# A decoder kernel on one core: dilation stage with its value step one tile later and stores on GpSimd; layer 1's output stage weighs a cached sequence at another place, with six slots

## The reference

```python
qb = to_res(q)                       # rows regrouped by residue mod d, blocks of 128
kk, vv = with_prev(to_res(k)), with_prev(to_res(v))   # own and previous block
s = jnp.einsum('brnqhe,brnkhe->brnhqk', qb, kk)
s = jnp.where(valid, s, NEG)         # rel >= 0 and rel <= window // d
m = jnp.max(s, axis=-1, keepdims=True)
p = jnp.exp(s - m)
l = jnp.sum(p, axis=-1, keepdims=True)
o = jnp.einsum('brnhqk,brnkhe->brnqhe', p / l, vv)
```

## Time and profile before

| what | value |
|---|---|
| median of 3 runs | 3226.03 us (3225.46 to 3228.44) |
| profiled execution, its own time | 3226.22 us |
| span in its trace, first to last instruction | 3224.6 us |
| mean granted TensorE clock | 0.974 of full speed |
| busy: TensorE, its weight loads, VectorE, ScalarE, GpSimd | 3021.1, 2481.6, 1254.7, 1036.8, 342.7 us |
| dilation stage, first load issued to first turn of the next stage | 2590.7 to 2886.4 us |
| layer 1's output stage, to the end | 2886.4 to 3224.6 us |

### The profile page before, as it was taken

One profiled execution on the slowest core, in us unless ns is written; L12 is line 12 of the kernel. 1 busy time (PEld: TensorE's weight loads), 2 busy tenths in 40 slices (PEclk: granted clock), 3 DMA queues, 4 the chain that ended last, 5 costly groups with the idle time before them and its releaser, 6 DMA issues. The chain is left out here.

```text
span 3224.6 us, 39799 instructions
## 1 busy us (share of the span) xinstructions
PE 3021.1 (94%) x14734; PEld 2481.6 (77%) x14734; DVE 1254.7 (39%) x2917; ACT 1036.8 (32%) x3236; POOL 342.7 (11%) x457
## 2 busy tenths in 40 slices
PE   7999999998997999979999999999889978869999
PEld 6788888886886888867888888888678767757777
DVE  4322222222335543344122222333332457756665
ACT  5211111111333242244021211333222357755642
POOL 0000000000110000000011011111332134430000
PEclk9999999999998999989999999999999989988999
DMA  4110111111234433142222221221663345554552
GB/s 141 37 40 30 40 32 37 37 32 37 88 131 155 143 133 102 66 146 88 69 76 69 72 73 68 75 74 67 155 170 124 125 143 176 185 179 158 188 172 94
DMA packets 159684, 324.88 MB, mean 101 GB/s; under 512 B 19184, under 2 KB 36144, under 8 KB 159528
## 3 DMA queue, kind: packets, MB, share of 16 engines
q1 hardware_dynamic: 136936, 253.25, 24.7%
q0 software_dynamic: 22592, 69.56, 6.2%
HBM read 223.58 MB, written 99.16 MB: 100 GB/s over the span
## 5 line engine op out<-in xcount | busy, mean ns | idle before, releaser
L109 PE MATMUL ps<-prepb_wh,b_xthi 128*128 128x512 f32 x784 | 309.6, 395 | 23.9 <-DVE tokb_o L878 15.3
L109 PE MATMUL ps<-b_wh,b_xthi 128*128 128x512 f32 x784 | 308.0, 393 | 6.7 <-DVE tokb_o L878 5.3
L110 PE MATMUL ps<-prepb_wl,b_xthi 128*128 128x512 f32 x784 | 307.5, 392 | 0.0
L111 PE MATMUL ps<-prepb_wh,b_xtlo 128*128 128x512 f32 x784 | 307.4, 392 | 0.0
L111 PE MATMUL ps<-b_wh,b_xtlo 128*128 128x512 f32 x784 | 306.4, 391 | 0.0
L110 PE MATMUL ps<-b_wl,b_xthi 128*128 128x512 f32 x784 | 306.3, 391 | 0.0
L786 ACT ACTIVATE tokb_o<-ps 128x128 f32<-128x128 f32 (+1 forms) x484 | 126.7, 276 | 437.2 <-PE ps L111 359.6
L109 PE MATMUL ps<-a_xthi,prepa_wh 128*128 128x512 f32 x512 | 200.6, 392 | 5.8 <-DVE prepa_wl L103 5.8
L109 PE MATMUL ps<-a_xthi,a_wh 128*128 128x512 f32 x512 | 201.1, 393 | 4.0 <-DVE a_xtlo L222 4.0
L110 PE MATMUL ps<-a_xtlo,prepa_wh 128*128 128x512 f32 x512 | 200.4, 391 | 0.0
L111 PE MATMUL ps<-a_xthi,prepa_wl 128*128 128x512 f32 x512 | 200.2, 391 | 0.0
(11 more groups left out here) (353 smaller groups left out, 6426.9 us busy)
## 6 DMA issues: line engine op xcount, KB each, us to landing
kv_dram<-tokb_o POOLq DMA_DIRECT2D x96, 256.0 KB, 2.3
tok_b_dram<-tokb_o POOLq DMA_DIRECT2D x96, 256.0 KB, 2.6
tokb_raw<-w_b_dram SPq DMA_DIRECT2D x88, 256.0 KB, 3.0
conv_raw<-w_a_dram SPq DMA_DIRECT2D x64, 256.0 KB, 3.4
grp_dram<-dil_o SPq DMA_DIRECT2D x48, 260.0 KB, 2.1
out_grp<-grp_dram SPq DMA_DIRECT2D x48, 260.0 KB, 4.3
dil_q<-tok_b_dram SPq DMA_DIRECT2D x48, 256.0 KB, 3.0
dil_k<-kv_dram SPq DMA_DIRECT2D x48, 256.0 KB, 3.5
```

Of the source, the lines that this page charges most:

```text
L109: pe.matmul(acc, a_hi, b_hi, start=first, stop=False)
L110: pe.matmul(acc, a_hi, b_lo, start=False, stop=False)
L111: return pe.matmul(acc, a_lo, b_hi, start=False, stop=last)
```

## The change

In the dilation stage:

- The value step comes one turn later: in the turn of s TensorE makes the scores of s-1, turns s, makes the sums of s-3 and turns the probabilities of s-2. ScalarE first makes the halves of q and k of s, then all exponentials of s-1, the copy of the sums of s-3, and the probabilities of s-2. VectorE makes the low probabilities of s-3, adds the sums of s-4, then all minima of s-1.
- SyncE only loads: q and k of s, then v of s-1. The stores are issued by GpSimd: in its body for tile s, after the value split of s, it waits for o_done of s-2 and stores tile s-2.
- VectorE's minima of a tile wait for the store of the tile four before, then for the scores, and begin with a memset of one column of a new small tile, once per half.

In layer 1's output stage:

- The ring has six slots (two new ones of 3 x 512 columns beside the four in the spare operands); the pair of t+1 is loaded in SyncE's iteration t.
- ScalarE weighs the first of pair t+1 between the exponentials and the high half of the turned probabilities of step t. Layer 0's output stage keeps its order.

The diff, without the list of semaphore names (which gains v_in4 and v_in5):

```diff
@@ -1023,7 +1023,6 @@
-    RING = 4
@@ -1035,6 +1034,7 @@
+        self.RING = 4 if self.conv else 6
 
@@ -1050,7 +1050,9 @@
         else:
+            ring = core.sb(st, f"{tag}_ring", [P, 2, 3, C])
             self.ring = [x[:, 3 * n:3 * n + 3, C:2 * C] for x in (spare0, spare1) for n in range(2)]
+            self.ring += [ring[:, n, :, :] for n in range(2)]
@@ -1422,7 +1424,7 @@
                 if conv and t < 4:
                     for j in (2 * t, 2 * t + 1):
                         keys.load(sp, j)
-                for v in pair_at(t):
+                for v in pair_at(t if conv else t + 1):
                     dec.load(sp, v)
                 if t == 0:
                     dec.small_loads(sp)
@@ -1492,12 +1494,14 @@
                     e = act.activation(prob[:, h, :], ps[:, 1 + h // 2, (h % 2) * MEM:(h % 2 + 1) * MEM], ACT.Exp,
                                        scale=SCALE, bias=stat[:, 1, h:h + 1], accum_out=stat[:, 2, h:h + 1])
                 e.then_inc(exped, 1)
+                for v in pair_at(t + 1)[:1] if not conv else ():
+                    dec.weigh(act, v)
                 act.wait_ge(pturned, t + 1)
                 act.activation(pt_hi, p_turned, ACT.Copy).then_inc(phi_done, 1)
                 if not conv:
                     act.wait_ge(mturned, t + 1)
                     act.activation(cat_hi[:, u, 0:H, :], turned_heads, ACT.Copy).then_inc(mhi_done, 1)
-                for v in pair_at(t + 1)[:1]:
+                for v in pair_at(t + 1)[:1] if conv else ():
                     dec.weigh(act, v)
             for t in range(NT):
                 step(t)
@@ -1861,6 +1865,7 @@
+        scratch = core.sb(st, "dil_scratch", [P, 2 * U])
@@ -1890,9 +1895,11 @@
 
         @block.sync
         def _(sp):
-            def store(s):
-                sp.wait_ge(o_done, cnt(s))
-                sp.dma_start(rows(dst[s[0]], *s), o_b[:, s[2], :]).then_inc(o_out[s[2]], 16)
+            def load_v(s):
+                g, _, u = s
+                if back(s, U):
+                    sp.wait_ge(vlo_done, cnt(back(s, U)))
+                sp.dma_start(v_b[:, u, :], rows(kv_src[g][:, C:2 * C], *s)).then_inc(v_in[u], 16)
 
             def body(*s):
                 g, _, u = s
@@ -1900,16 +1907,10 @@
                     sp.wait_ge(turned, cnt(back(s, U)))
                 sp.dma_start(q_b[:, u, :], rows(q_src[g], *s)).then_inc(qk_in[u], 16)
                 sp.dma_start(k_b[:, u, :], rows(kv_src[g][:, 0:C], *s)).then_inc(qk_in[u], 16)
-                if back(s, U):
-                    sp.wait_ge(vlo_done, cnt(back(s, U)))
-                sp.dma_start(v_b[:, u, :], rows(kv_src[g][:, C:2 * C], *s)).then_inc(v_in[u], 16)
-                if back(s, 3):
-                    store(back(s, 3))
+                if back(s, 1):
+                    load_v(back(s, 1))
             turns(sp, body)
-            for k in (3, 2, 1):
-                store(back(END, k))
-            for s in o_out:
-                sp.wait_ge(s, 16 * TURNS * GROUPS)
+            load_v(back(END, 1))
 
         @block.gpsimd
         def _(pool):
@@ -1920,6 +1921,10 @@
                 cols = masks[:, at * P:(at + 1) * P]
                 pool.affine_select(out=cols, in_=cols, compare_op=ALU.is_ge, fill=NEG, base=0,
                                    pattern=[[-sign, P]], channel_multiplier=sign).then_inc(masked, 1)
+
+            def store(s):
+                pool.wait_ge(o_done, cnt(s))
+                pool.dma_start(rows(dst[s[0]], *s), o_b[:, s[2], :]).then_inc(o_out[s[2]], 16)
 
             def body(*s):
                 u = s[2]
@@ -1932,7 +1937,13 @@
                 pool.wait_ge(vhi_done, cnt(s))
                 pool.tensor_tensor(v_hl[:, slot, :, 1, :], v, v_hl[:, slot, :, 0, :], ALU.subtract
                                    ).then_inc(vlo_done, 1)
+                if back(s, 2):
+                    store(back(s, 2))
             turns(pool, body)
+            for k in (2, 1):
+                store(back(END, k))
+            for s in o_out:
+                pool.wait_ge(s, 16 * TURNS * GROUPS)
 
         @block.scalar
         def _(act):
@@ -1956,41 +1967,45 @@
                 act.wait_ge(pturned, half_cnt(s, half))
                 act.activation(pt_hi[:, heads, a:b, :], turned_p[:, heads, a:b, :], ACT.Copy).then_inc(phi_done, 1)
 
+            def probs(s):
+                for half in range(2):
+                    probs_high(s, half)
+
             def body(*s):
-                one = back(s, 1)
-                if one:
-                    exps(one, 0)
+                one, two, three = (back(s, k) for k in (1, 2, 3))
                 act.wait_ge(turned, cnt(s))
                 act.activation(qt_hi[:, :], ps[:, 0, :], ACT.Copy).then_inc(qhi_done, 1)
                 act.activation(kt_hi[:, :, s[2] % 2, :], ps[:, 5, :].rearrange("p (h k) -> p h k", h=H), ACT.Copy
                                ).then_inc(khi_done, 1)
                 if one:
+                    exps(one, 0)
                     exps(one, 1)
-                    probs_high(one, 0)
-                    probs_high(one, 1)
-                if back(s, 2):
-                    copy_sums(back(s, 2))
+                if three:
+                    copy_sums(three)
+                if two:
+                    probs(two)
             turns(act, body)
-            last = back(END, 1)
-            for half in range(2):
-                exps(last, half)
-            for half in range(2):
-                probs_high(last, half)
-            copy_sums(back(END, 2))
-            copy_sums(last)
+            one, two, three = (back(END, k) for k in (1, 2, 3))
+            exps(one, 0)
+            exps(one, 1)
+            copy_sums(three)
+            probs(two)
+            copy_sums(two)
+            probs(one)
+            copy_sums(one)
 
         @block.vector
         def _(dve):
-            def wait_scores(s, half):
-                dve.wait_ge(scored, half_cnt(s, half))
-                if half == 0 and back(s, U):
-                    dve.wait_ge(o_out[s[2]], use(back(s, U)))
-
             def minima(s, half):
+
                 a, b = span(s)
                 u, slot = s[2], s[2] % 2
+                if half == 0 and back(s, U):
+                    dve.wait_ge(o_out[u], use(back(s, U)))
+                dve.wait_ge(scored, half_cnt(s, half))
+                dve.memset(scratch[:, 2 * u + half:2 * u + half + 1], 0.0)
                 for h in (2 * half, 2 * half + 1):
                     m = dve.tensor_tensor_reduce(
                         prob[:, slot, h, a:b, :].rearrange("p s k -> p (s k)"),
@@ -2013,16 +2028,13 @@
                 dve.tensor_tensor(o, sums_hl[:, :, 1, :], o, ALU.add).then_inc(o_done, 1)
 
             def attend(s):
-                one, two, three = (back(s, k) for k in (1, 2, 3))
-                for half in range(2):
-                    if one:
-                        wait_scores(one, half)
-                    if two:
-                        probs_low(two, half)
-                    if one:
-                        minima(one, half)
-                    if three and half == 0:
-                        add_sums(three)
+                one, three, four = (back(s, k) for k in (1, 3, 4))
+                for half in range(2 if three else 0):
+                    probs_low(three, half)
+                if four:
+                    add_sums(four)
+                for half in range(2 if one else 0):
+                    minima(one, half)
 
             def body(*s):
                 attend(s)
@@ -2034,11 +2046,11 @@
             dve.wait_ge(masked, 3)
             turns(dve, body)
             attend(END)
-            last = back(END, 1)
-            for half in range(2):
-                probs_low(last, half)
-            add_sums(back(END, 2))
-            add_sums(last)
+            for k in (2, 1):
+                for half in range(2):
+                    probs_low(back(END, k), half)
+                add_sums(back(END, k + 1))
+            add_sums(back(END, 1))
 
         @block.tensor
         def _(pe):
@@ -2091,19 +2103,22 @@
                         t.then_inc(pturned, 1)
 
             def body(*s):
-                if back(s, 1):
-                    score(back(s, 1))
+                one, two, three = (back(s, k) for k in (1, 2, 3))
+                if one:
+                    score(one)
                 turn(s)
-                if back(s, 2):
-                    sums(back(s, 2))
-                if back(s, 1):
-                    turn_probs(back(s, 1))
+                if three:
+                    sums(three)
+                if two:
+                    turn_probs(two)
             turns(pe, body)
-            last, before = back(END, 1), back(END, 2)
-            score(last)
-            sums(before)
-            turn_probs(last)
-            sums(last)
+            one, two, three = (back(END, k) for k in (1, 2, 3))
+            score(one)
+            sums(three)
+            turn_probs(two)
```

(9 more changed lines are left out.)

## The result

The changed kernel takes **3295.65 us** (median of four runs, 3291.33 to 3302.84) against 3226.97 (3225.46 to 3228.44): a ratio of 1.0215, 95% interval 1.0195 to 1.0236. The forecast was 3246 and its range ended at 3280: the sign was right, the size wrong. The profiled run took 3291.33 us with a span of 3289.7, 65.1 us over the span of before.

What follows compares the result with a forecast made beforehand. The prediction took GpSimd's store behind the value split, holding VectorE's minima, to bound the dilation stage. From 3226.2 us it added 35.4 for that stage and took off 16 for the output stage: 3246, range 3212 to 3280.

Steps and rivals of the forecast that it cites:

- Part 1: Dilation stage: SyncE keeps only loads, so TensorE's 17.4 us of key-load waits can go; reordering wins 0.3 us a full step.
- the ring of 5.8 us: Dilation stage: VectorE and ScalarE work in order, minima to addition and minima again, 5.8 us a full step against 6.1.
- rival C: Dilation stage: the store never holds the minima and the stage runs at 5.8 us a full step; 3196 us, chance 0.12.
- Part 2: Dilation stage: GpSimd's store, issued behind the value split, holds up VectorE's minima; +35 us together with the drain.
- L: Dilation stage: issue and landing of GpSimd's store, taken as 3.1 us; bounds 2.1 and 3.9, each microsecond worth 21 us.
- the prediction's own formulas: Dilation stage: 10.9 us plus the store's landing for two full steps, 8.6 plus the landing for two short ones.
- D: Dilation stage: TensorE's new waits lower its clock, about 2.5 us in half of 21 double steps; +26, 3272 us, chance 0.13.
- Part 3: Layer 1's output stage: weighing fits ScalarE's gap, TensorE's 13.6 us of waits go; -16 us, bounds -8 and -21.

Runs made afterwards that it cites:

- store-first kernel: The changed kernel with GpSimd's store moved ahead of its wait for the sums and the value split: 3197.51 us, 0.9908 of the kernel before.
- the run with the later loads: The changed kernel with SyncE's key and value loads released by VectorE's query half of two tiles back, value load one turn later: 3279.88 us, 1.0172 of the kernel before.

## Why the prediction was wrong in size

**Part 1 held.** The waits for key loads are gone, and the ring of 5.8 us is what the store-first kernel runs in (92.66/16 = 5.79 in group 0). That kernel is the case of rival C, the store off the path: 3196 was its price, 3197.5 is measured, though its short steps take 5.1 us (76.58/15) where C had 4.7. But it is not the lead of the loads alone that shortens a full step: without the extra step those of group 0 take 6.1 (97.42/16).

**Part 2: VectorE's wait for the store came as forecast; L was mis-sized.** VectorE waits at the memset for the store, and moving the store alone removes the loss. With L = 4.0 instead of 3.1 the prediction's own formulas give two full steps in 14.9 us and two short ones in 12.6: +14.2, +19.2, +15.6 and 5 for the drain, +54 in place of +35. That is 19 us of the miss, and by itself it would give 3265, inside the range. L was put midway between a store alone and one beside two loads; here three loads start within 1.4 us of it, and the row with company (3.9) was the near one. The same store lands in 2.3 when it leaves 2.0 us ahead of the loads. The fit of the Trainium skill (DMA: Bandwidth & Descriptors, section Anatomy of one DMA) was cited for 2.6; the trace comes near it, with 2.3, only for a store with a head start. The same page of the Trainium skill (section SWDGE vs HWDGE vs iDMA) says that a DMA engine takes turns between GpSimd's queue and SyncE's, which fits these landings, though no run here shows the turns themselves.

**The clock was a term of the sum put at nothing, and TensorE's work was left off the path.** This is the step that takes the time out of the range. By the formula with L = 4.0 groups 0, 1, 2 and the drain should be 14.2, 19.2, 15.6 and 5 us longer; they are 17.5, 24.4, 33.1 and 9.4. So 30 us more are missing, 17.5 of them in group 2. There TensorE is busy 82.40 us against 62.49, at a clock of 0.76. In the double step shown, score, turn and sums take 6.28 us at 0.50; in the next turn, at the full level, the score takes 1.38 (2927.23 to 2928.61), the turn 1.06 (2928.61 to 2929.67) and the sums to GpSimd's next start 1.27 (2930.00 to 2931.27), 3.71 together. That is 2.57 us. In the three double steps ahead of it the same piece takes 6.12, 5.87 and 5.91 us, 2.2 to 2.4 too long, so 7.5 double steps lose 16 to 19 us: an estimate from these rows, for the 17.5 missing.

The prediction followed only the path by way of the exponentials and probabilities, where TensorE has little work. The ring shown above, minima to low halves to score, turn and sums, costs 2.33 + 3.71 + 2.56 + 4.0 = 12.6 us at the full clock, the same as the first, and takes the half clock in full. D was priced at 26 with a chance of 0.13, as another way and not as an addition. Added to 3265 its 26 gives the measured time, and that is partly luck: D spread 2.5 us over half of all double steps, and most of what is missing lies in group 2. Its "against", that group 1 with waits of a microsecond stays at 1.00, compared waits of another length: in the changed kernel they are up to 5.3 us. The Trainium skill (TensorE: Matmul & The Clock Gate, section HAM oscillation — how this bites in real kernels) tells of such a pattern, a wait for data between short stretches of matmuls that start at the half clock every time; this trace agrees, with 0.50 after a wait of 3.5 us.

That the clock is the cause of group 2's part is read from rows and was not isolated: no run fills TensorE's waits with other matmuls. Two comparisons speak for it. Group 2 takes 85.86 us with the store between the split's operations and 76.58 with the store first, 9.3 apart, and TensorE's busy time there is 9.8 apart (73.43 and 63.65), at clocks of 0.84 and 0.98 (VectorE's waits for the store are 5.3 us apart, 7.6 and 2.3). And in the run with the later loads the landing of group 2 was 0.8 us shorter while its excess over the formula stayed near 17 us (25.4 longer than before, where L = 3.1 gives 8.9), at 0.77. The 13 us that are missing in groups 0 and 1 and in the drain are given to no cause.

**Part 3: the size nearly right, the cause wrong.** -16 was forecast, -20.7 is what the full change won in this stage (65.1 less 85.8, by which its first step comes later), at the end of the bound of -21. But the sum gave it to the weighing's place in ScalarE's gap. TensorE's 13.6 us came from landings inside the weighing. The waits of ScalarE in steps 3 to 10 of the kernel before say so, 27.2 us together:

```profile
ACT b_spare L1223 <- DMA b_spare<-dil_v_dram: 14.6, 4, 5.1
ACT b_spare L1223 <- DMA b_spare<-cache_v_dram: 12.6, 4, 4.2
```

The row of L1223 in the earlier trace rows has the first of them, and it was read for its 28.9 us of work only. The new place alone costs 47 us.

**The sum again.** 3246, plus 19 for L, plus 30 beyond the formula, less 5 for the output stage is 3290, against 3291.3 for the profiled run. It closes because the 30 are what the windows have beyond the formula; they are no independent sum. Of them 16 to 19 are priced from rows, as said.

## What to carry to other kernels

A store that frees a buffer belongs ahead of the waits of its queue, not behind the work that the same step happens to bring; ask what stands in front of it and which loads the same event releases. When a change lengthens TensorE's waits, price the clock as a term of the sum, on every path that holds TensorE's work. Where an engine idles before an operation, read what ended the idle time before moving the operation: here a late load was mended by an earlier load, with a buffer for it.

## What the runs showed of the chip

A 260-KB store from GpSimd landed in 2.3 us with 2.0 us of head start on SyncE's loads and in 4.0 beside three of them; issuing it took 0.56 us of GpSimd's time, against 0.36 of SyncE's in the kernel before and 0.34 of ScalarE's. The one-column memset took 0.06 us. After waits of 3.5 us TensorE came back at 0.50 of its clock and did 3.7 us of work in 6.3. With waits for the low half of at most 1.8 us group 2 stood at 0.84 (the store between the split's operations) and at 0.91 (the store from ScalarE), and with waits of at most 1.7 at 0.98 (the store first); we have no reading of why these differ so much.
